# An eight-core hybrid encoder layer: the per-head norm of the recurrence output moved between attention blocks, and preparation code rewritten as generators

## What is computed

```python
def token_mixers(n, positions, w_in, ...):
    proj = n @ w_in
    q_r, fz_f, fz_b, i_r, g_r, q_a, k_a, v_a, gate_r, gate_a = jnp.split(proj, SPLIT_IDX, axis=-1)
    ...
    o = o_f + o_b
    o = (o * lax.rsqrt(jnp.mean(o * o, axis=-1, keepdims=True) + NORM_EPS)
         * hg_norm.astype(f32).reshape(HG_HEADS, HG_VAL_DIM))
    o = o.reshape(B, S, HG_VW) * jax.nn.silu(g_r.astype(f32))
    y_rec = o.astype(n.dtype) @ w_br_rec
    ...
    y_att = window_gqa_sink(qa, ka, va, sink) @ w_br_att
    merged = jax.nn.sigmoid(gate_r) * y_rec + jax.nn.sigmoid(gate_a) * y_att
    return merged @ w_out
```

## Time and profile before

| | |
|---|---|
| median of 2 runs | 4346.14 us (4341.89 and 4350.39) |
| profiled execution | 4341.66 us, span of its slowest core 4340.4 us |
| spans of the eight cores | 4323.1 to 4340.4 us |
| mean granted TensorE clock of the cores | 0.778 to 0.788 |
| busy over the span: PE, DVE, ACT | 72%, 47%, 32% |

### The profile page before, as it was taken

The page is one execution under the profiler, slowest core; times in us unless marked ns, Lnnn a source line. Parts: engine busy times, 40 slices in busy tenths (PEclk is TensorE's granted clock), DMA queues, the critical chain, the costliest instruction groups (busy, mean ns, idle before and its releaser), DMA issues.

```text
span 4340.4 us, 51205 instructions; the slowest of 8 cores (4323.1 to 4340.4 us)
## 1 busy us (share of the span) xinstructions
PE 3130.5 (72%) x15216; PEld 1481.3 (34%) x15216; DVE 2023.1 (47%) x4160; ACT 1380.6 (32%) x2484; POOL 31.2 (1%) x61
## 2 busy tenths in 40 slices
PE   2555566666788578858875897589678957895887
PEld 1323333333333233333333333333333433343333
DVE  1343444444354436453735473547344643555363
ACT  2233333433332332242224232322232233324222
POOL 1000000000000000000000000000000000000000
PEclk7666666667799679968986998599868977996898
DMA  7889832223223222422241234033312432232233
GB/s 149 166 157 167 161 106 96 94 92 129 82 91 120 94 88 88 136 76 97 104 149 37 107 111 151 30 109 127 123 58 94 151 100 74 91 130 82 92 110 120
DMA packets 93070, 470.85 MB, mean 108 GB/s; under 512 B 9604, under 2 KB 9732, under 8 KB 59524
## 3 DMA queue, kind: packets, MB, share of 16 engines
q1 hardware_dynamic: 86756, 424.86, 28.8%
q0 software_dynamic: 6048, 42.73, 7.3%
HBM read 468.34 MB, written 84.67 MB: 127 GB/s over the span
## 4 chain that ended last, share of the span: by engine, by line
PE 50%; DVE 21%; issue 9%; DMA 9%; ACT 8%; DVEq 1%; SPq 0%; ACTq 0%; POOL 0%; POOLq 0%
PE ps L589 36%; DMA sb_xt<-x 4%; DVE sb_PF L1004 2%; DVE sb_X L1026 2%; DVE sb_PF L1043 2%; PE ps L718 2%; PE ps L722 2%; DMA sb_posi<-pos 2%; PE ps L621 2%; DMA out<-sb_ot 1%; PE ps L560 1%; DVE sb_nT L582 1%; ACT sb_PT L918 1%; PE ps L914 1%; DVE sb_PF L1042 1%
## 5 line engine op out<-in xcount | busy, mean ns | idle before, releaser
L589 PE MATMUL ps<-sb_nT,sb_wring 128*128 128x512 bf16 (+1 forms) x6208 | 1486.5, 396 | 157.9 <-DVE sb_nT L582 78.8
L589 PEld LDWEIGHTS ps<-sb_nT,sb_wring 128*128 128x128 bf16 x6208 | 618.4, 101 | 1007.0 <-issue 366.0
L589 PE MATMUL ps<-sb_X,sb_wring 128*128 128x512 bf16 x2432 | 576.7, 395 | 67.5 <-DVE sb_X L1011 30.7
L589 PEld LDWEIGHTS ps<-sb_X,sb_wring 128*128 128x128 bf16 x2432 | 243.4, 101 | 390.4 <-issue 130.9
L573 ACT ACTIVATE sb_B<-sb_hT 128x512 bf16<-128x512 f32 (+2 forms) x272 | 153.0, 604 | 556.1 <-DVE sb_hT L1057 271.5
L560 PE MATMUL ps<-sb_con,sb_xt 128*128 128x128 f32 x512 | 107.8, 388 | 247.2 <-DMA sb_xt<-x 232.2
L582 DVE SCALAR_TENSOR_TENSOR sb_nT<-sb_hT,sb_par,sb_PF 128x512 bf16<-128x512 f32 (+1 forms) x200 | 132.6, 734 | 320.0 <-ACT sb_PF L580 320.0
L685 PE MATMUL ps<-sb_identb,sb_X 128*128 128x128 bf16 x256 | 37.5, 301 | 289.0 <-DVE sb_X L672 289.0
L699 ACT ACTIVATE sb_S<-sb_U,sb_gam 128x128 bf16<-128x128 f32 x504 | 162.5, 390 | 191.1 <-DVE sb_U L728 122.1
L1038 ACT COPY sb_gs<-ps 128x512 f32<-128x512 f32 x176 | 103.2, 586 | 285.6 <-PE ps L589 285.6
L1025 ACT ACTIVATE sb_PF<-sb_PF 128x512 f32<-128x512 f32 x176 | 110.9, 630 | 220.9 <-DVE sb_PF L1044 220.7
(11 more groups left out here) (169 smaller groups left out, 3467.9 us busy)
## 6 DMA issues: line engine op xcount, KB each, us to landing
sb_wring<-wscr SPq DMA_DIRECT2D x204, 1024.0 KB, 5.5
sb_wring<-wscr SPq DMA_DIRECT2D x72, 704.0 KB, 4.1
sb_wring<-wscr SPq DMA_DIRECT2D x64, 768.0 KB, 4.2
wscr<-wall POOLq DMA_DIRECT2D x40, 1024.0 KB, 12.5
sb_xt<-x SPq DMA_DIRECT2D x64, 512.0 KB, 4.6
out<-sb_ot SPq DMA_DIRECT2D x62, 256.0 KB
ntscr<-sb_nT SPq DMA_DIRECT2D x8, 1024.0 KB, 7.5
obscr<-sb_HG SPq DMA_DIRECT2D x8, 1024.0 KB, 7.6
```

Of the source, the lines that this page charges most:

```text
L589: S.op("pe", lambda e, o=o, k=k: e.matmul(ps[:, 0:N], wt[:, o:o + 128], rhs(k), start=(k == 0), stop=(k == nk - 1)), reads=[bwt, brhs[k]], ...
```

## The change

It has five parts.

1. The norm of the recurrence output becomes a function `o_norm(hd)`. The loop over the four heads between the recurrence and the attention is gone; instead `o_norm(qb)` is called at the end of attention block `qb`, behind the copy of its transposed result. The operations in it are the same.
2. The silu of the output gate is kept in `B8[:, 4 + hd]` instead of `X1[:, OA + hd]`, since the attention's copy writes `X1[:, OA:OA + 4]` before the norm reads the gate.
3. `rmsnorm` on a full tile keeps its reciprocal root in a buffer of its own, `rstd`, and the ring of temporaries `PF` has 6 entries instead of 7.
4. `load_x_tile` and `rmsnorm` become generators with wrappers that run them to the end at once, and the first pass calls the new wrapper `p1_prep`.
5. `hgrn_tile` takes a new argument `bg`, a generator that it would advance twice per chunk. No call passes one.

```diff
--- before.py
+++ after.py
@@ -375,7 +375,7 @@
     nT = sb("nT", [128, KC, T], BF16); bn = bufs("n", KC)
     B8 = sb("B8", [128, KC, T], BF16); bB = bufs("B", KC)
     X1 = sb("X1", [128, JF, T], BF16); bX = bufs("X", JF)
-    NPF = 7
+    NPF = 6
     PF = sb("PF", [128, NPF, T], F32); bPF = bufs("pf", NPF)
     HG = sb("HG", [128, 3, 4, T], F32); bHG = [bufs(f"hg{i}_", 4) for i in range(3)]
     KT = sb("KT", [128, 2, SEQ], BF16); bKT = bufs("kt", NT)
@@ -403,6 +403,7 @@
     wring = sb("wring", [128, NSLOT, SLOT], BF16); bring = bufs("ring", NSLOT)
     posi = sb("posi", [128, T], I32); bposi = S.buf("posi")
     rot = sb("rot", [128, 2, T], F32); brot = bufs("rot", 2)
+    rstd_t = sb("rstd", [128, T], F32); brstd = S.buf("rstd")
     nint = sb("nint", [128, T], I32); bnint = S.buf("nint")
     gcar = sb("gcar", [128, JF, 2], F32); bgcar = bufs("gcar", JF)
     ucar = sb("ucar", [128, JF], F32); bucar = bufs("ucar", JF)
@@ -546,7 +547,7 @@
         x_dma(ti, 1)
         xpre["tile"] = ti
 
-    def load_x_tile(ti, nxt=None):
+    def load_x_tile_gen(ti, nxt=None):
         have = xpre["tile"] == ti
         xpre["tile"] = None
         for blk in range(4):
@@ -564,23 +565,37 @@
                     ps[:, :].rearrange("p (a b) -> p a b", a=4)), reads=[bps], writes=bh[half * 4:half * 4 + 4])
             if blk >= 2 and nxt is not None:
                 x_dma(nxt, blk - 2)
-        if nxt is not None:
-            xpre["tile"] = nxt
+            if blk == 3 and nxt is not None:
+                xpre["tile"] = nxt
+            yield
+
+    def load_x_tile(ti, nxt=None):
+        for _ in load_x_tile_gen(ti, nxt):
+            pass
 
     def rmsnorm(src, bsrc, gname, N, out, bout, nk=KC, ones=None):
+        for _ in rmsnorm_gen(src, bsrc, gname, N, out, bout, nk, ones):
+            pass
+
+    def rmsnorm_gen(src, bsrc, gname, N, out, bout, nk=KC, ones=None):
         ones = onesD if ones is None else ones
         for k in range(nk):
             S.op("act", lambda e, k=k: e.activation(B8[:, k, 0:N], src(k), AF.Square), reads=[bsrc[k]], writes=[bB[k]])
+        yield
         ps, bps = psum_next()
         for k in range(nk):
             S.op("pe", lambda e, k=k: e.matmul(ps[:, 0:N], ones[:], B8[:, k, 0:N], start=(k == 0), stop=(k == nk - 1)),
                  reads=[bB[k], bcst], writes=[bps], inc=(k == nk - 1))
-        rs, brs = tmpf()
+        yield
+        rs, brs = (rstd_t[:, :], brstd) if N == T else tmpf()
         S.op("act", lambda e: e.activation(rs[:, 0:N], ps[:, 0:N], AF.Ln, bias=sm[:, 40:41]), reads=[bps, bsm], writes=[brs])
         S.op("act", lambda e: e.activation(rs[:, 0:N], rs[:, 0:N], AF.Exp, scale=-0.5), reads=[brs], writes=[brs])
+        yield
         for k in range(nk):
             S.op("dve", lambda e, k=k: e.scalar_tensor_tensor(out(k), src(k), pr(gname, k, k + 1), rs[:, 0:N], ALU.mult, ALU.mult),
                  reads=[bsrc[k], brs, bpar], writes=[bout[k]])
+            if k % 4 == 3:
+                yield
 
     def proj_F(wt, bwt, blk, rhs, brhs, N, nk=KC, wstride=None):
         ps, bps = psum_next()
@@ -597,7 +612,7 @@
     bvs = bufs("vs", NT)
     bnts = bufs("nts", NT)
 
-    def hgrn_tile(ti, d, first, mid_hook=None):
+    def hgrn_tile(ti, d, first, mid_hook=None, bg=None):
         tok0 = ti * T
         wt, bwt = ring_next("fzf" if d == 0 else "fzb")
         sgs = []
@@ -728,16 +743,28 @@
                     S.op("dve", lambda e, hd=hd: e.scalar_tensor_tensor(U[:, hd, :], U[:, hd, :], gam[:, hd, c:c + 1], psU[:, hd * 128:(hd + 1) * 128],
                                                                         ALU.mult, ALU.add),
                          reads=[bU[hd], bgam, bpsU], writes=[bU[hd]])
+            if bg is not None:
+                next(bg, None)
+                next(bg, None)
+        if bg is not None:
+            for _ in bg:
+                pass
         return held
 
     bob = bufs("ob", NT)
+    def p1_prep_gen(ti):
+        yield from load_x_tile_gen(ti, nxt=(ti - 1 if ti > 0 else None))
+        yield from rmsnorm_gen(lambda k: hT[:, k, H0:H0 + T], bh, "g_mix", T, nTk, bn)
+        S.dma("sp", nts_d[ti], nT[:], reads=bn, writes=[bnts[ti]])
+        yield
+
+    def p1_prep(ti):
+        for _ in p1_prep_gen(ti):
+            pass
+
     for idx, ti in enumerate(range(NT - 1, -1, -1)):
         tok0 = ti * T
-        load_x_tile(ti, nxt=(ti - 1 if ti > 0 else None))
-        rmsnorm(lambda k: hT[:, k, H0:H0 + T], bh, "g_mix", T, nTk, bn)
-        S.dma("sp", nts_d[ti], nT[:], reads=bn, writes=[bnts[ti]])
-        if idx == 0:
-            tap("nT1", nT[:], bn, [128, KC, T])
+        p1_prep(ti)
         S.dma("sp", posi[:], pos_d[:, tok0:tok0 + T].partition_broadcast(128), writes=[bposi])
         posf, bposf = tmpf()
         S.op("dve", lambda e: e.tensor_copy(posf, posi[:]), reads=[bposi], writes=[bposf])
@@ -864,7 +891,7 @@
             wt, bwt = ring_next("gr")
             for hd in range(4):
                 psg, bpsg = proj_F(wt, bwt, hd, nTk, bn, T)
-                S.op("act", lambda e, hd=hd: e.activation(X1[:, OA + hd, :], psg[:, :], AF.Silu), reads=[bpsg], writes=[bX[OA + hd]])
+                S.op("act", lambda e, hd=hd: e.activation(B8[:, 4 + hd, :], psg[:, :], AF.Silu), reads=[bpsg], writes=[bB[4 + hd]])
             for jj in range(2):
                 wt, bwt = ring_next(f"qq{jj}")
                 for sub in range(2):
@@ -885,19 +912,16 @@
         psum_release(held)
         if ti == 0:
             tap("osum", HG[:, KK], bHG[KK], [128, 4, T])
-        rss = []
-        for hd in range(4):
-            S.op("act", lambda e, hd=hd: e.activation(B8[:, hd, :], HG[:, KK, hd, :], AF.Square), reads=[bHG[KK][hd]], writes=[bB[hd]])
+        def o_norm(hd):
+            S.op("act", lambda e: e.activation(B8[:, hd, :], HG[:, KK, hd, :], AF.Square), reads=[bHG[KK][hd]], writes=[bB[hd]])
             ps, bps = psum_next()
-            S.op("pe", lambda e, hd=hd: e.matmul(ps[:, :], onesV[:], B8[:, hd, :], start=True, stop=True), reads=[bB[hd], bcst], writes=[bps])
+            S.op("pe", lambda e: e.matmul(ps[:, :], onesV[:], B8[:, hd, :], start=True, stop=True), reads=[bB[hd], bcst], writes=[bps])
             rs, brs = tmpf()
             S.op("act", lambda e: e.activation(rs, ps[:, :], AF.Ln, bias=sm[:, 40:41]), reads=[bps, bsm], writes=[brs])
             S.op("act", lambda e: e.activation(rs, rs, AF.Exp, scale=-0.5), reads=[brs], writes=[brs])
-            S.op("dve", lambda e, hd=hd: e.tensor_tensor(rs, rs, HG[:, KK, hd, :], ALU.mult), reads=[brs, bHG[KK][hd]], writes=[brs])
-            S.op("dve", lambda e, hd=hd: e.scalar_tensor_tensor(X1[:, OG + hd, :], rs, pr("hgn", hd, hd + 1), X1[:, OA + hd, :], ALU.mult, ALU.mult),
-                 reads=[brs, bX[OA + hd], bpar], writes=[bX[OG + hd]])
-        if ti == 0:
-            tap("og", X1[:, OG:OG + 4, :], bX[OG:OG + 4], [128, 4, T])
+            S.op("dve", lambda e: e.tensor_tensor(rs, rs, HG[:, KK, hd, :], ALU.mult), reads=[brs, bHG[KK][hd]], writes=[brs])
+            S.op("dve", lambda e: e.scalar_tensor_tensor(X1[:, OG + hd, :], rs, pr("hgn", hd, hd + 1), B8[:, 4 + hd, :], ALU.mult, ALU.mult),
+                 reads=[brs, bB[4 + hd], bpar], writes=[bX[OG + hd]])
         if ti == 0:
             tap("qrT", X1[:, QR:QR + 4, :], bX[QR:QR + 4], [128, 4, T])
         for qb in range(4):
@@ -954,6 +978,9 @@
                      reads=[boatok[osl], bcst], writes=[bps], inc=(kc == 3))
             S.op("act", lambda e: e.copy(X1[:, OA:OA + 4, qb * 128:(qb + 1) * 128], psb[:, 0:512].rearrange("p (a b) -> p a b", a=4)),
                  reads=[bps], writes=bX[OA:OA + 4])
+            o_norm(qb)
+        if ti == 0:
+            tap("og", X1[:, OG:OG + 4, :], bX[OG:OG + 4], [128, 4, T])
         if ti == 0:
             tap("oaT", X1[:, OA:OA + 4, :], bX[OA:OA + 4], [128, 4, T])
         for j in range(8):
```

## The result

| | before | changed |
|---|---|---|
| median of all runs | 4384.73 us (12 runs, 4339.36 to 4619.20) | 4456.33 us (14 runs, 4361.14 to 4676.94) |
| undisturbed runs | six, 4339.36 to 4362.44 us, middle 4346.8 | six, 4361.14 to 4378.76 us, middle 4365.3 |
| ratio of undisturbed runs | 1 | 1.0044, 95% interval 1.0023 to 1.0066 |
| the same in a second comparison, on one chip | 1 | 1.0053, interval 1.0033 to 1.0073 |

In about half of the executions of either kernel (36 of 66 before, 11 of 20 changed, over all comparisons) the cores of one die or of both have a lower mean granted TensorE clock, down to 0.69 where it is mostly 0.77 to 0.79, and the run is up to 7% longer, so every ratio here is one of the other, undisturbed runs.

What follows compares the result with a forecast made beforehand. No engine was full: an engine-to-engine chain from DVE sums to the norm's readers was the bound. Per tile -10.53 + 3 x 3.92 + 2.21 = +3.44 us, times 8 = +27.5, on 4341.7 gave 4369.2, stated as 4371 us; range 4350 to 4390.

Steps and rivals of the forecast that it cites:

- The time: Whole kernel: new median between 4369 and 4374 us, said as 4371, with runs' median 4.5 us above the profiled execution.
- The norm ahead of block 0: From DVE sums to block 0's transposes: scores no longer follow the norm on PE, 10.53 us saved per tile.
- The bank: Block 0's first scores wait for PSUM banks that DVE must have read in the sums; the third sum ends at 1924.37.
- The boundary: Between attention blocks: one head's norm delays the next first mask from +1.81 to +5.73, 3.92 us at each of three.
- The end: Behind block 3: the merge loop's first matmul starts 2.59 us behind the transposes instead of 0.38, 2.21 us lost.
- The cover: Merge loop: the last norm ends about 5.73 us behind the transposes, before its reader at +7.24, hidden by sixteen projections.
- The sum: Per tile -10.53 + 3 x 3.92 + 2.21 = +3.44 us, times 8 tiles = +27.5 us.
- The edits costed at nothing: Silu in `B8`, ring of six, `rmsnorm`'s own buffer, generators and unused `bg`: no cost anywhere in the kernel.
- The norm hides in the blocks: Rival, attention blocks: idle ACT and DVE absorb the norm, boundaries and end cost nothing, -84 us, 4257 us; chance 0.07.
- Table loads: Rival, block boundaries: two loads of 1.28 us each if `Exp` and `Ln` differ in set, 61 us more, 4431; chance 0.03.
- The clock rises later: Rival, merge loop: PE's higher clock comes later, 2.2 us per tile, 18 us, 4387; chance 0.08.
- The clock rises inside the attention: Rival, attention blocks: PE's clock rises there, saving 9 us per tile, 4297; chance 0.02.

Runs made afterwards that it cites:

- e3_rest_only: The changed kernel with the norm back ahead of the attention and the gate's silu back in `X1`; ratio 0.9997 to the kernel before.
- e5_hoist: The changed kernel with each head's square, matmul, `Ln` and `Exp` issued in the idle time at its block's end; ratio 0.9824 to the kernel before.
- e8_all_end: The changed kernel with all four norms behind the fourth attention block, ahead of the merge loop; ratio 0.9995 to the kernel before.

## Why the prediction was right in its sum and wrong in its time

**The time, wrong.** The step that failed is the last one of the sum: "The runs' median lies 4.5 us above that execution, so the new median should lie between 4369 and 4374". It took two runs, 4341.89 and 4350.39, for the spread of this kernel. With ten more, the kernel before itself has a median of 4384.73 and runs up to 4619.20. My range of 4350 to 4390 was built from the kernel's mechanisms alone and had no term for that. What the term is worth is the distance of the median of all runs from the middle of the undisturbed ones: 4384.73 - 4346.8 = 38 us before and 4456.33 - 4365.3 = 91 us for the changed kernel, against the 4.5 us that I took. So the forecast of 4371 us met 4456.33.

What a trace shows in place of the missing term is a lower granted clock outside the stage of the change. These are the windows from the end of the sixth tile's stage (the start of the matmuls on the norm's result) to the seventh's sums, first in the kernel before, then in the changed kernel's execution of 4476.36 us (core 5):

```profile
3225.40:3579.20 353.80, 289.10 (x1296) 130.62 (x1294) 181.33 (x354) 101.43 (x174) 0.20 (x1) 0.87 0.34 119
3273.60:3651.60 378.00, 322.64 (x1296) 140.08 (x1294) 182.89 (x355) 99.59 (x173) 0.20 (x1) 0.77 0.32 111
```

The same 1296 matmuls take 33.5 us more of PE and the stretch 24.2 us more, at 0.77 for 0.87. Four tiles earlier the same stretch of this execution, 1571.80 to 1923.20, takes 351.4 us at 0.87, and over its eight tiles the stage of the change has a mean of 63.9 us. So the time was lost elsewhere than in the stage of the change. In its slowest core the clock stands at 0.81 for some 1020 us in all, most of it in stretches where PE has hardly a gap (139 us from 3406 on, PE busy for 137.3); in the kernel before's profiled execution, with the same work, it is never at this level. Why it comes in one execution and not in the next was not tried, and stays open.

**The norm ahead of block 0, right.** Predicted 10.53 us saved, measured 22.89 - 12.11 = 10.78. The bank was the cause of the scores' wait: predicted start at +2.13, measured +2.02 with DVE's sum as releaser, and +0.22 once other banks were handed out. The first mask came 0.2 us earlier than predicted.

**The boundary, right.** Predicted +3.92, measured 3.95, 3.82 and 3.84. The square's result reached PE in 0.77 us (1951.53 - 1950.76) where I had taken 0.86 from a row; the rest, 3.66 us from the matmul to the mask, came out to the hundredth (1955.19 - 1951.53).

**The end, 0.3 us too dear.** Predicted 2.21, measured 2.32 - 0.38 = 1.94, for the same 0.09, for 0.05 by which the copy came sooner, and because the projection follows the norm's matmul in 0.39 us (1996.31 - 1995.92 in this tile) and not in the 0.52 of the scores. The cover held: the norm's reader came 2.67 us behind the last product in this tile, and with the shortest projections of the 64 tiles (4.56 us) it would still have come 1.2 us behind it. The 2.4 us from the start of the projections to the higher clock, which I had read from one tile, are near the least: the mean over the 64 tiles is 3.9 us.

**The sum.** Predicted +3.44 us a tile, measured -10.78 + 11.61 + 1.94 = +2.77, times eight +22 against +27.5. The surplus of 5.5 us is three small terms that all fell on one side: 0.25 at the start, 0.15 at the boundaries, 0.27 at the end. None of them touches the mechanism. I had also taken 2% for the least that a measurement of this kernel can tell; the interval of the undisturbed runs is 0.2% to either side, and tells the 0.4%.

**The edits costed at nothing, right** (e3_rest_only, 0.9997).

**The rivals.** *The norm hides in the blocks*: not in this change, but its condition was the right one. A boundary below 2.8 us was to gain, and where the boundary is 0.2 to 0.3 us (e5_hoist) the kernel is 76 us faster; this rival's price of 84 us for full hiding was hardly off. *Table loads*: none in the stage; the first is the sigmoid's at 2000.00, as before. The Trainium skill (ScalarE: Activation LUTs, "Table sets: the hidden batching unit") says that `ln` and `exp` share a set, and the trace agrees for the new order too: `Ln`, the norm's `Exp` and the attention's follow each other at 1952.22, 1953.00 and 1953.54 without a load. *The clock rises later*: in the tile shown above it did, 5.1 us behind the start of the projections where it was 2.4, and they took 6.0 us instead of 4.65. But over all 64 tiles the projections take only 0.12 us more than before, 1 us in all, where this rival asked for 18; and a start 10 us later in e8_all_end did no more. *The clock rises inside the attention*: 0.50 in both windows.

## What to carry to other kernels

An in-order queue sees a chain only where the code issues it: to hide a dependent chain of small operations, issue each step where its engine is idle and its operand is ready, not the whole chain at one point between two stages. Moving the unchanged chain from one place with nothing beside it to four such places cost 22 us here, and the same operations issued a few lines earlier gained about 76 against the kernel before. Look at each step by its engine, too: between two heads' scores the norm's matmul on PE cost 0.43 us of a block, and the steps on ACT and DVE nothing. Before forecasting an absolute time, ask how many runs stand behind the median, and forecast the ratio beside it.
